# Crossbar DMA transposes from DRAM in place of TensorE transposes, and another last tile, in an eight-core conformer layer

## The chip, the cores and the metric

One program runs on the 8 cores of a Trainium2 chip. Each core has its own engines: TensorE (PE, with its weight loads as PEld), VectorE (DVE), ScalarE (ACT), GpSimd (POOL) and SyncE (SP), and 16 DMA engines that all queues share. The metric is the device time of the slowest core in microseconds (us); the median over the runs counts.

## The reference

One layer over `x` of shape (2, 8192, 1024):

```
u = rms_norm(x, g);  a_val | a_gate | q | k | v = u @ W_in
A = silu(layer_norm(conv31(a_val * sigmoid(a_gate))))        # 512 channels
B = attention(q, k, v)      # 8 heads x 64; a 64-frame chunk sees itself and the 8 chunks before it,
                            # with a learned bias by distance
x = x + rms_norm(concat(A, B) @ W_out)
f = (gelu(gate) * val) @ W_down,  gate | val = conv3(rms_norm(x) @ W_up)    # width 2816
x = x + rms_norm(f)
```

## The kernel before

Each core computes 2048 tokens and reads 640 tokens ahead of them again, so it holds 21 token tiles (`w` = 0 to 20) of 128 tokens. The tiles form groups `g`: 0 (tiles 0 to 3), 1 (tile 4), 2 (5 to 8), 3 (9 to 12), 4 (13 to 16) and 5 (17 to 20). Groups 2 to 5 are the core's own tokens.

The program has these stages. A start projects groups 0 to 2 while the weights arrive. Then come four attention slots, one for each group 2 to 5; in each, the 20 steps of the group's attention (`attn_steps`: scores, exponential, values) are woven with other work: normalizing and transposing the tiles of later groups (`prep_a`, `prep_b`), projecting them (`proj_a`, `proj_v`, `proj_k`, `proj_q`), the 31-wide convolution (`conv_units`), its layer norm (`ln_units`), and in the last slot the output projection of the first half (`wo_step`). Then the FFN runs in two halves `H`, each an up part (`ffn`) and a down part (`ffn_down`) over 8 tiles.

A matmul contracts over partitions, so activations must be channel-major before they meet a weight. Two places turn them. `prep_b(w)` takes the normalized tile `ub` (128 tokens x 1024 channels, bf16), does eight 128x128 TensorE transposes into a PSUM bank (L561) and one DVE copy into `uT` (L565). `fin(n)`, four per slot, takes the attention output of one token tile out of `atok`, does four TensorE transposes (L845) and one DVE copy into `aoT` (L849); `wo_mm` reads `aoT` as its stationary operand.

All operations are recorded with their reads and writes, and a list scheduler orders them for each engine by a priority, which is the order of recording, and by estimated durations. `weave` records the side work of a slot at given fractions of the attention steps; those pairs of numbers in `slot` set the order. The order is then fixed: each engine and each queue issues its instructions in that order and waits at each for its semaphores. SP issues nearly all plain DMAs (x tiles L498, the convolution's input out to DRAM and back as `hd`, L701 and L708, and others), one queue in one order; a DMA on SP whose source is not ready holds all that stand behind it.

The last tile of the second half has a routine of its own, `last()`: it multiplies the left 512 output columns over all 22 weights first (L1204), so that their squares (L1207) are taken while the right 512 columns run, and it sends the result as two halves on two queues (L1224). All other tiles go through `part` (both halves together, L1172) and `epi` (squares over 1024 columns L1188, two GpSimd operations for the reciprocal root, L532 and L535, two DVE operations L1191 and L1194, one DMA L1195).

Of the kernel before, what the change touches and what calls it, by code (L numbers as in the profile page):

```python
# [9 lines left out]
BF16 = mybir.dt.bfloat16  # L10
# [10 lines left out]
AFF = 0  # L21
AHEAD = 0
CWF = 0.8
# [297 lines left out]
def build_program():  # L321
# [23 lines left out]
    hd = {g: nc.dram_tensor("hd%d" % g, [8, 128, 4 * GS[g]], BF16).ap() for g in GS}  # L345
    CN = {0: 129, 1: 128}
# [3 lines left out]
    with ExitStack() as es:  # L350
# [17 lines left out]
        def pb(name, b0, nb=1, dt=F32):  # L368
# [6 lines left out]
            ["h1s", "wob"] + ["hd%d" % g for g in GS] + ["cd0", "cd1"])}  # L375
# [25 lines left out]
        assert o <= 16740, o  # L401

        uTb = {i: sb("uT%d" % i, 16740 + i * 8192, [8, 512], BF16) for i in range(2)}
        u2T = sb("u2T", 16740, [8, 1028], BF16)
        Wk = sb("Wk", 33188, [8, 512], BF16)
        Wv = sb("Wv", 41380, [8, 512], BF16)
        Wo = sb("Wo", 33188, [8, 1024], BF16)
        Wq = sb("Wq", 49572, [8, 512], BF16)
        coT = [sb("coT%d" % i, 49572, [4, 1032], BF16) for i in range(2)]
        sig = [sb("sig%d" % i, 57828 + i * 2048, [512]) for i in range(2)]  # L410
        hst = [sb("hst%d" % i, (61924, 153284)[i], [8, 4, 64], BF16) for i in range(2)]
# [7 lines left out]
        aoT = [sb("aoT0", 113316, [4, 1026], BF16), sb("aoT1", 57828, [4, 1024], BF16)]  # L419
# [13 lines left out]
        uT4 = sb("uT4", 195876, [8, 128], BF16)  # L433
# [36 lines left out]
        PL = [pb("PL%d" % i, 4 + i) for i in range(2)]  # L470
# [86 lines left out]
        def prep_b(w):  # L557
            u_ = ub[w % 3]
            b = nbank(True)
            for k in range(8):  # L560
# [3 lines left out]
            ut, j = uT_of(w)  # L564
            S.op("dve", lambda: dve.tensor_copy(out=ut.ap[:, :, j * 128:(j + 1) * 128],  # L565
                                                in_=b.apb.rearrange("p (k t) -> p k t", k=8)),
# [27 lines left out]
        def proj_v(g, j):  # L594
# [3 lines left out]
            for k in range(8):  # L598
                S.mm(lambda k=k: pe.matmul(b.ap, lhsT=ut.ap[:, k, j * 128:(j + 1) * 128], rhs=Wv.ap[:, k, :],  # L599
                                           start=(k == 0), stop=(k == 7)),  # L600
                     reads=[ut[j], Wv[(k, 0)]], writes=[b], last=(k == 7))
# [7 lines left out]
        def v_wide():  # L609

            bs = [nbank() for _ in range(5)]
            for k in range(8):
                for w in range(5):
                    ut, j = uT_of(w)
                    S.mm(lambda k=k, w=w, ut=ut, j=j: pe.matmul(bs[w].ap, lhsT=ut.ap[:, k, j * 128:(j + 1) * 128], rhs=Wv.ap[:, k, :],  # L615
# [11 lines left out]
        def k_wide():  # L627
# [3 lines left out]
            for k in range(8):  # L631
                for c in range(4):
                    S.mm(lambda k=k, c=c: pe.matmul(bs[c].ap, lhsT=Wk.ap[:, k, c * 128:(c + 1) * 128], rhs=ut.ap[:, k, :],
# [18 lines left out]
        def proj_k(g, c):  # L652
# [4 lines left out]
            for k in range(8):  # L657
                S.mm(lambda k=k: pe.matmul(b.ap[:, :N], lhsT=Wk.ap[:, k, c * 128:(c + 1) * 128], rhs=ut.ap[:, k, :N],  # L658
# [7 lines left out]
        def proj_q(g, c):  # L666
# [4 lines left out]
            for k in range(8):  # L671
                S.mm(lambda k=k: pe.matmul(b.ap[:, n0:N], lhsT=Wq.ap[:, k, c * 128:(c + 1) * 128], rhs=ut.ap[:, k, n0:N],  # L672
# [4 lines left out]
        def proj_a(g, c, part):  # L677
# [7 lines left out]
            for k in range(8):  # L685
                S.mm(lambda k=k: pe.matmul(b.ap[:, :n], lhsT=Wa.ap[:, k, col:col + 128], rhs=ut.ap[:, k, n0:N],  # L686
# [5 lines left out]
            else:  # L692
                s_ = n // 8
                S.op("dve", lambda: dve.scalar_tensor_tensor(
                    out=hs.ap[:, :, c, 0:s_], in0=sg.ap[:, :n].rearrange("p (s q) -> p q s", q=8), scalar=1.0,
                    in1=b.ap[:, :n].rearrange("p (s q) -> p q s", q=8), op0=ALU.add, op1=ALU.mult),
# [16 lines left out]
        def halo_units():  # L713
# [39 lines left out]
            def turn():  # L753
                b = nbank()
                for c in range(4):
# [3 lines left out]
                S.op("dve", lambda: dve.tensor_copy(out=aoT[0].ap[:, :, 0:2], in_=b.apb[:, 0:8].rearrange("p (c t) -> p c t", c=4)),  # L759
                     reads=[b], writes=[aoT[0][4]])  # L760
# [405 lines left out]
        def ffn_down(H):  # L1166
# [63 lines left out]
            for i in range(8):  # L1230
# [17 lines left out]
                if H and i == 7:  # L1248
                    last()
                    continue  # L1250
# [10 lines left out]
            if H == 0:  # L1261
                epi(7)
# [270 lines left out]
```

The softmax here doesn't subtract the row's maximum and nothing guards it: scores larger than these inputs give would overflow.

## Time and profile before

| what | value |
|---|---|
| median of 3 runs | 842.96 us (841.79 to 843.06) |
| the profiled execution | 841.79 us |
| span of its slowest core (core 3), first to last instruction | 840.7 us |
| spans of all cores | 834.7 to 840.7 us |
| PE busy | 790.6 us, 94% |
| DVE busy | 588.2 us, 70% |
| ACT busy | 499.9 us, 59% |
| POOL busy | 179.7 us, 21% |

The profiled execution took 1.1 us more than its span. Busy shares are averages over the whole span; the stages have different limits. The attention slots lie between about 65 and 335 us, the FFN from 335 us on.

### The profile page before, as it was taken

To read this page: it belongs to the slowest core of one execution; us is meant where nothing else is said; L and a number is where in the kernel's file an instruction comes from. 1 tells how busy PE (TensorE), PEld (TensorE's weight loads), DVE (VectorE), ACT (ScalarE), POOL (GpSimd) and SP (SyncE) were. 2 spreads that over 40 slices of the span, in tenths; PEclk is the share of its full clock that TensorE was granted. 3 is DMA by queue.
4 is the path that set the end of the run, shared out by engine and by line. 5 is a ranking of instruction groups with operands and counts; after the bars stand their busy time and mean duration, and the time that the engine had idled before them with its cause. 6 is when DMAs were issued, how large, how long until landed. Compare 5 with 4: busy or idle time off the path is not lost.

```text
span 840.7 us, 15580 instructions; the slowest of 8 cores (834.7 to 840.7 us)
## 1 busy us (share of the span) xinstructions
PE 790.6 (94%) x5324; PEld 420.1 (50%) x5324; DVE 588.2 (70%) x758; ACT 499.9 (59%) x764; POOL 179.7 (21%) x324
## 2 busy tenths in 40 slices
PE   1998998899998897999999999999999999999997
PEld 1545465554554445666666654444444444444443
DVE  2566477778757888889999984454488888885223
ACT  4567363525555787789888784323377777772111
POOL 3122121000003453232333311111222222200010
PEclk9999999999999999999999999999999999999999
DMA  8994778021637843599999995443398888811222
GB/s 258 310 292 133 126 151 101 27 44 9 127 92 129 166 157 102 60 101 107 111 113 114 181 147 159 153 161 139 126 153 78 78 76 80 77 15 50 102 101 101
DMA packets 145619, 101.00 MB, mean 120 GB/s; under 512 B 117122, under 2 KB 124674, under 8 KB 145156
## 3 DMA queue, kind: packets, MB, share of 16 engines
q0 software_dynamic: 95520, 31.37, 36.7%
q1 hardware_dynamic: 49444, 68.29, 27.8%
q8 instruction: 44, 0.72, 0.4%
q14 instruction: 35, 0.29, 0.1%
q10 hardware_dynamic: 576, 0.34, 0.1%
HBM read 110.31 MB, written 23.12 MB: 159 GB/s over the span
## 4 chain that ended last, share of the span: by engine, by line
PE 73%; DVE 13%; issue 7%; ACT 5%; DMA 1%; POOL 1%; DVEq 0%; ACTq 0%; POOLq 0%
PE ps L1277 24%; PE ps L1172 14%; PE ps L686 7%; PE ps L1088 5%; DVE big L1299 4%; DVE big L1302 4%; PE ps L672 3%; PE ps L599 3%; PE ps L658 3%; PE ps L920 2%; PE ps L790 2%; PE ps L826 2%; PE ps L615 1%; PE ps L1204 1%; PE ps L561 1%
## 5 line engine op out<-in xcount | busy, mean ns | idle before, releaser
L1277 PE MATMUL ps<-big 128*128 128x344 bf16 (+2 forms) x1760 | 310.9, 337 | 1.1 <-ACT big L1298 0.9
L1277 PEld LDWEIGHTS ps<-big 128*128 128x128 bf16 x1760 | 171.2, 98 | 139.8 <-issue 3.9
L1172 PE MATMUL ps<-big 128*128 128x512 bf16 x660 | 144.2, 378 | 0.0
L1299 DVE SCALAR_TENSOR_TENSOR big<-big 128x1026 f32<-128x1026 f32 (+1 forms) x88 | 113.0, 1285 | 20.3 <-ACT big L1289 11.2
L1163 POOL DMA_DIRECT2D big<-w_up x88 | 77.4, 880 | 213.0 <-PE ps L1277 192.4
L1302 DVE SCALAR_TENSOR_TENSOR big<-big 128x1026 f32<-128x1026 f32 (+1 forms) x88 | 113.3, 1288 | 9.4 <-DVE big L1299 0.7
L1294 ACT ACTIVATE big<-ps,big 128x1026 f32<-128x1026 f32 (+1 forms) x88 | 106.8, 1214 | 0.0
L1172 PEld LDWEIGHTS ps<-big 128*128 128x128 bf16 x660 | 63.7, 97 | 76.6
L801 ACT ACTIVATE big<-ps 128x1024 bf16<-128x1024 f32 x80 | 80.2, 1024 | 26.9 <-PE ps L790 22.3
L1088 PE MATMUL ps<-big 128*128 128x512 bf16 (+1 forms) x272 | 64.9, 391 | 2.1 <-DVE big L1036 2.1
L1290 ACT COPY big<-ps 128x1024 f32<-128x1024 f32 x44 | 44.6, 1015 | 36.1 <-PE ps L1277 36.0
L535 POOL TENSOR_TENSOR big<-big 128x1 f32<-128x1 f32 (+1 forms) x71 | 50.3, 710 | 71.3 <-DVE big L1105 55.4
L686 PE MATMUL ps<-big 128*128 128x512 bf16 (+1 forms) x320 | 61.4, 340 | 3.9 <-ACT big L690 1.8
L1191 DVE SCALAR_TENSOR_TENSOR big<-ps,big 128x1024 f32<-128x1024 f32 x15 | 19.3, 1285 | 62.7 <-POOL big L535 62.7
L532 POOL TENSOR_SCALAR big<-big 128x1 f32<-128x1 f32 (+1 forms) x53 | 16.7, 315 | 189.3 <-ACT big L1188 86.4
L1312 DVE TENSOR_TENSOR big<-big 128x1026 bf16<-128x1026 bf16 (+1 forms) x44 | 53.7, 1221 | 0.3 <-ACT big L1099 0.2
L1283 ACT COPY big<-ps 128x1032 f32<-128x1032 f32 x44 | 44.5, 1011 | 15.7 <-PE ps L1277 8.7
L1188 ACT ACTIVATE big<-ps 128x1024 bf16<-128x1024 f32 x15 | 15.3, 1023 | 57.9 <-PE ps L1172 57.9
L1309 ACT ACTIVATE big<-big 128x1026 bf16<-128x1026 f32 (+1 forms) x44 | 46.7, 1061 | 4.7 <-DVE big L1302 2.4
L813 POOL MEMSET big<- 64x128 bf16 x64 | 14.6, 229 | 147.4 <-ACT big L801 95.6
L1126 ACT ACTIVATE big<-big 128x1024 bf16<-128x1024 f32 (+1 forms) x17 | 18.0, 1061 | 46.4 <-DVE big L1114 46.0
L1088 PEld LDWEIGHTS ps<-big 128*128 128x128 bf16 (+1 forms) x272 | 25.9, 98 | 34.7 <-issue 6.3
(126 smaller groups left out, 934.2 us busy)
## 6 DMA issues: line engine op xcount, KB each, us to landing
big<-w_up POOLq DMA_DIRECT2D x88, 256.0 KB, 5.4
big<-xw SPq DMA_DIRECT2D x37, 512.0 KB, 6.6
big<-w_in SPq DMA_DIRECT2D x40, 256.0 KB, 12.3
h1s<-big SPq DMA_DIRECT2D x16, 512.0 KB, 2.9
big<-h1s SPq DMA_DIRECT2D x16, 512.0 KB, 5.1
out<-big SPq DMA_DIRECT2D x15, 512.0 KB, 2.9
big<-w_down POOLq DMA_DIRECT2D x22, 256.0 KB, 6.1
hd<-big SPq DMA_DIRECT2D x4, 512.0 KB, 3.4
```

The costliest lines, as they stand in the source:

```text
L535: S.op("pool", lambda: pool.tensor_tensor(out=stat.ap[0:n, out:out + 1], in0=stat.ap[0:n, tmp:tmp + 1], in1=nh.ap[0:n], op=ALU.pow), reads ...
L686: S.mm(lambda k=k: pe.matmul(b.ap[:, :n], lhsT=Wa.ap[:, k, col:col + 128], rhs=ut.ap[:, k, n0:N], start=(k == 0), stop=(k == 7)), reads=ut ...
L801: S.op("act", lambda: act.activation(out=p_.ap, in_=s_.ap, func=AF.Exp), reads=[s_], writes=[p_], n=1024)
L1088: S.mm(lambda k=k, half=half, l_=l_, b=b: pe.matmul(b.ap[0:n], lhsT=l_, rhs=Wo.ap[:, k, half * 512:(half + 1) * 512], start=(k == 4), stop ...
L1163: S.dma("pool", "wup%d" % (si % NWR), lambda: pool.dma_start(out=wring[si % NWR].ap, in_=w_up_v[:, :, cbk * 128:(cbk + 1) * 128]), writes= ...
L1172: S.mm(lambda f=f, half=half, i=i: pe.matmul((PH[2] if i % 2 else PD).ap[:, half, :], lhsT=actb[f].ap[:, i * 128:(i + 1) * 128], rhs=Wd[f] ...
L1277: S.mm(lambda k=k, t=t, c0=c0, n_=n_: pe.matmul(pu.ap[:, t, 0:n_], lhsT=wb.ap[:, k, :], rhs=u2T.ap[:, k, c0:c0 + n_], start=(k == 0), stop ...
L1294: S.op("act", lambda: act.activation(out=tav, in_=pv, func=AF.Identity, scale=fdw.ap[:, cbk, 2:3], bias=fdw.ap[:, cbk, 3:4]), reads=[pu, f ...
L1299: S.op("dve", lambda: dve.scalar_tensor_tensor(out=tbv, in0=xv[1], scalar=fdw.ap[:, cbk, 1:2], in1=tav, op0=ALU.mult, op1=ALU.add), reads= ...
L1302: S.op("dve", lambda: dve.scalar_tensor_tensor(out=tav, in0=xv[0], scalar=fdw.ap[:, cbk, 0:1], in1=tbv, op0=ALU.mult, op1=ALU.add), reads= ...
L1309: S.op("act", lambda: act.activation(out=av_, in_=tav, func=AF.Gelu_apprx_tanh), reads=[ta], writes=[actb[j]], n=1026)
L1312: S.op("dve", lambda: dve.tensor_tensor(out=av_, in0=av_, in1=tav, op=ALU.mult), reads=[ta, actb[j]], writes=[actb[j]], n=1026)
```

## The change

Four things change together.

1. `prep_b` of tiles 9 to 20 (groups 3 to 5, `TD = 9`) no longer uses PE and DVE. SP stores the normalized tile to a DRAM tensor `ud` (256 KB) and then reads it back with one DMA crossbar transpose into `uT`. Tiles 0 to 8 stay as they were.
2. `fin` runs once per head pair instead of once per token tile: SP stores the 512 x 128 outputs of that pair to a DRAM tensor `at` (128 KB) and reads them back with a crossbar transpose into `aoT`, which is now one buffer per group. There are 16 such pairs.
3. So that a transposed tile lands in one piece, `uT` is laid out by tile, then channel block, then token. The moving operand of `proj_k`, `proj_q` and `proj_a` is now four runs of 128 elements in place of one run of 512.
4. `last()` is gone: the last tile goes through `part` and `epi` like the others.

Smaller edits: of each four `affine` operations of the first layer norm two go to ACT (`AFF = 2`); every second `proj_a` product is read in order and written strided instead of the other way round; and the fractions in `slot` are all new.

```diff
-AFF = 0
+AFF = 2
+TD = 9
+TKB = 768
...
-        uTb = {i: sb("uT%d" % i, 16740 + i * 8192, [8, 512], BF16) for i in range(2)}
+        uTb = {i: sb("uT%d" % i, 16704 + i * 8192, [4, 8, 128], BF16) for i in range(2)}
...
         def prep_b(w):
             u_ = ub[w % 3]
+            ut, j = uT_of(w)
+            if w >= TD:
+                S.dma("sp", "ud%d" % (w % 3), lambda: sp.dma_start(out=ud[w], in_=u_.ap), reads=[u_], writes=[DH["ud%d" % w]], kb=256)
+                S.dma("sp", "ut%d" % (w % 3), lambda: sp.dma_start_transpose(out=ut.ap[:, j, :, :], in_=ud[w]),
+                      reads=[DH["ud%d" % w]], writes=[ut[j]], kb=TKB)
+                return
             b = nbank(True)
...
-                S.mm(lambda k=k: pe.matmul(b.ap[:, :N], lhsT=Wk.ap[:, k, c * 128:(c + 1) * 128], rhs=ut.ap[:, k, :N],
+                S.mm(lambda k=k: pe.matmul(b.ap[:, :N].rearrange("p (a b) -> p a b", b=128), lhsT=Wk.ap[:, k, c * 128:(c + 1) * 128], rhs=ut.ap[:, :, k, :],
...
+                o_, r_ = hs.ap[:, :, c, 0:s_], "p (s q) -> p q s"
+                if c % 2:
+                    o_, r_ = o_.rearrange("p q s -> p s q"), "p (s q) -> p s q"
...
-            def fin(n):
-                b = nbank()
-                for c in range(4):
-                    S.mm(lambda c=c: pe.transpose(out=b.apb[:, c * 128:(c + 1) * 128],
-                                                  in_=atok.ap[:, n - n0, c * 128:(c + 1) * 128], identity=ident.ap),
-                         reads=[atok[h_] for h_ in range(4)] + [ident], writes=[b], last=(c == 3), n=140)
...
+            def fin(hp):
+
+                S.dma("sp", "ao%d" % (hp % 2), lambda: sp.dma_start(out=atd[g, hp].rearrange("(n p) c -> p n c", p=128),
+                                                                    in_=atok.ap[:, :, hp * 128:(hp + 1) * 128]),
+                      reads=[atok[hp]], writes=[DH["at%d%d" % (g, hp)]], kb=192)
+                S.dma("sp", "at%d" % (hp % 2), lambda: sp.dma_start_transpose(out=aoT[g].ap[:, hp, :], in_=atd[g, hp]),
+                      reads=[DH["at%d%d" % (g, hp)]], writes=[aoT[g][hp]], kb=TKB / 2)
...
-                if H and i == 7:
-                    last()
-                    continue
...
-                         (pa_units(1) + pa_units(2), 0, 0.19), (prep_units(3), 0.061, 0.179),
...
+                         (pa_units(1) + pa_units(2), 0, 0.19), (prep_units(3), 0.066, 0.288),
...
```

What this does to the order is seen on two engines. The rows are those of the program, not of a trace: a line number, an operation, its tiles and how often it repeats. First SP's queue at the start of the slot of group 2, before; `xw` are x tiles, `cvp` and `fdw` small constants, `hd` the convolution's input (the 128x8x16 and 128x32x4 forms are those of group 1).

```order
L514 DMA big<-w_in 128x512 x8
L498 DMA big<-xw 128x1024 x3
L1385 DMA big<-cvp 128x96
L1388 DMA big<-fdw 128x176
L498 DMA big<-xw 128x1024
L701 DMA hd<-big 128x8x16
L708 DMA big<-hd 128x32x4
L498 DMA big<-xw 128x1024 x3
```

The same queue in the changed kernel, from the end of the small constants on. The first row's two transposes are those of tiles 9 and 10, the next that of tile 11, the last that of tile 12.

```order
L566 DMA_TRANSPOSE big<-ud 128x8x128 x2
L712 DMA hd<-big 128x8x16
L566 DMA_TRANSPOSE big<-ud 128x8x128
L502 DMA big<-xw 128x1024
L565 DMA ud<-big 128x1024
L502 DMA big<-xw 128x1024
L565 DMA ud<-big 128x1024
L502 DMA big<-xw 128x1024
L565 DMA ud<-big 128x1024
L719 DMA big<-hd 128x32x4
L566 DMA_TRANSPOSE big<-ud 128x8x128
```

Between the store of group 1's convolution input and its way back (L712 and L719) there are now a transpose, three x loads and three stores, and the transpose of tile 12 stands behind all of them. The stores of tiles 9 to 11 and the two small constants come ahead of these rows.

Now PE, where group 3's tiles are first used; before, L686 is `proj_a` (L694 after), L561 the transposes of `prep_b`, L790 and L826 scores and values (L801 and L837 after), L741 the values of the halo (L752 after). Before, the last row below holds the last 8 matmuls of group 2 and all 64 of group 3.

```order
L686 MATMUL ps<-big 128x512 x16
L561 MATMUL ps<-big 128x128 x8
L826 MATMUL ps<-big 128x65 x4
L790 MATMUL ps<-big 128x512 x2
L790 MATMUL ps<-big 128x128 x2
L790 MATMUL ps<-big 128x384 x2
L686 MATMUL ps<-big 128x512 x16
L561 MATMUL ps<-big 128x128 x8
L826 MATMUL ps<-big 128x65 x8
L686 MATMUL ps<-big 128x512 x72
```

In the changed kernel group 2's last 8 `proj_a` matmuls come in the fourth row; L607 is `proj_v`, on tiles 9 and 10, and the last row is `proj_a` on group 3, which reads all four tiles.

```order
L694 MATMUL ps<-big 128x512 x56
L752 MATMUL ps<-big 2x65 x20
L837 MATMUL ps<-big 128x65 x8
L752 MATMUL ps<-big 2x65 x20
L694 MATMUL ps<-big 128x512 x8
L837 MATMUL ps<-big 128x65 x8
L767 MATMUL ps<-big 128x2 x4
L801 MATMUL ps<-big 128x512 x2
L801 MATMUL ps<-big 128x128 x2
L801 MATMUL ps<-big 128x384 x2
L837 MATMUL ps<-big 128x65 x8
L607 MATMUL ps<-big 128x512 x16
L694 MATMUL ps<-big 128x512 x16
```

The transposes are gone from PE, and 16 `proj_v` matmuls and the halo's values now stand ahead of group 3's first `proj_a`.

## Rows read from the trace of the kernel before

**Rows 1.** The page's chain that ended last: shares of the span by engine.

```profile
PE 73%; DVE 13%; issue 7%; ACT 5%; DMA 1%; POOL 1%; DVEq 0%; ACTq 0%; POOLq 0%
```

**Rows 2.** Busy us by engine in four stretches (PE, PEld, DVE, ACT, POOL), clock, DMA.

```profile
65.00:160.00 95.00, 86.27 (x908) 50.98 (x907) 60.29 (x104) 52.86 (x82) 17.21 (x47) 0.98 0.59 107
160.00:220.00 60.00, 59.55 (x433) 30.15 (x431) 49.13 (x110) 26.41 (x36) 2.72 (x13) 1.00 0.21 45
220.00:262.00 42.00, 40.38 (x418) 24.49 (x415) 26.14 (x47) 21.58 (x32) 2.04 (x10) 1.00 0.52 115
262.00:335.30 73.30, 62.03 (x602) 33.61 (x596) 60.98 (x109) 56.73 (x93) 35.30 (x59) 0.94 0.65 141
```

**Rows 3.** Timeline of PE in slots 2 and 3: start us, us, engine, line.

```profile
91.10 15.85 PE L686 MATMUL ps<-big 128*128 128x512 bf16 x72 [1.02 <-ACT big L690]
...
157.75 0.40 PE L845 MATMUL ps<-big 128*128 128x128 bf16 x4
157.99 0.61 PE L561 MATMUL ps<-big 128*128 128x128 bf16 x8
158.43 0.40 PE L826 MATMUL ps<-big 128*128 128x65 bf16 x8
...
180.13 1.90 PE L599 MATMUL ps<-big 128*128 128x512 bf16 x8
181.87 1.90 PE L686 MATMUL ps<-big 128*128 128x512 bf16 x8
```

**Rows 4.** Groups by line: busy us, mean ns of one, idle before.

```profile
L845 PE MATMUL ps<-big 128*128 128x128 bf16 x64 | 5.4, 219 | 3.0 <-DVE big L1102 1.4 <-DVE big L849 1.1 <-ACT big L675 0.5
```

**Rows 5.** Timeline of SP's queue in the slot of group 2.

```profile
69.89 0.42 SPq L1388 DMA_DIRECT2D big<-fdw  x1
...
80.70 0.64 SPq L708 DMA_DIRECT2D big<-hd  x1
```

**Rows 6.** The eight loads of `wob` (256 KB each, one row of 2 KB per partition).

```profile
DMA to landing us min/median/max: 2.8/6.2/7.2
```

**Rows 7.** The five loads of `hd` (four of 512 KB in runs of 128 B).

```profile
DMA to landing us min/median/max: 6.4/7.4/9.4
```

**Rows 8.** The page's DMA issues: KB each, median us to landing.

```profile
out<-big SPq DMA_DIRECT2D x15, 512.0 KB, 2.9
big<-hd SPq DMA_DIRECT2D x1, 32.0 KB, 6.4
```

**Rows 9.** Timeline of the end: tile 14's `epi`, then `last()`.

```profile
825.50 9.66 PE L1204 MATMUL ps<-big 128*128 128x512 bf16 x44
826.16 1.03 ACT L1188 ACTIVATE big<-ps 128x1024 bf16<-128x1024 f32 x1 [8.68 <-PE ps L1172]
...
831.31 0.34 SPq L1195 DMA_DIRECT2D out<-big  x1
...
835.30 0.60 ACT L1207 ACTIVATE big<-ps 128x512 bf16<-128x512 f32 x1 [4.00 <-PE ps L1204]
...
838.62 0.35 ACTq L1224 DMA_DIRECT2D out<-big  x1
```

**Rows 10.** Groups by line, shapes kept apart, on DVE and ACT.

```profile
L565 DVE COPY big<-ps 128x1024 bf16<-128x1024 bf16 x21 | 14.2, 689 | 11.0 <-PE ps L561 11.0
L849 DVE COPY big<-ps 128x512 bf16<-128x512 bf16 x16 | 6.3, 422 | 5.5 <-PE ps L845 5.1
L694 DVE SCALAR_TENSOR_TENSOR big<-big,ps 128x512 bf16<-128x512 f32 x16 | 17.3, 1079 | 18.7 <-PE ps L686 16.5 <-ACT big L551 1.1 <-PE ps L826 1.0
L837 DVE TENSOR_TENSOR big<-ps,big 128x512 bf16<-128x512 f32 x16 | 11.0, 685 | 0.4
L997 DVE TENSOR_SCALAR big<-big 128x129 f32<-128x129 f32 x32 | 9.4, 343 | 0.0
L994 ACT ACTIVATE big<-big 128x128 f32<-128x128 f32 x32 | 14.2, 493 | 4.5 <-DVE big L987 4.5
```

**Rows 11.** PE and PEld busy us of line L561 alone, in one stretch.

```profile
160.00:220.00 60.00, 0.97 (x15) 0.72 (x12) 1.00 0.21 45
```

More of the change, by code:

```diff
@@ L345, in build_program @@
     hd = {g: nc.dram_tensor("hd%d" % g, [8, 128, 4 * GS[g]], BF16).ap() for g in GS}
+    ud = {w: nc.dram_tensor("ud%d" % w, [128, D], BF16).ap() for w in range(TD, NT)}
+    atd = {(g, c): nc.dram_tensor("at%d%d" % (g, c), [512, 128], BF16).ap() for g in range(2, 6) for c in range(4)}
     CN = {0: 129, 1: 128}
@@ L374, in build_program @@
         DH = {k: Buf(S, "dram", k, i, i + 1, None) for i, k in enumerate(
-            ["h1s", "wob"] + ["hd%d" % g for g in GS] + ["cd0", "cd1"])}
+            ["h1s", "wob"] + ["ud%d" % w for w in range(TD, NT)] + ["at%d%d" % (g, c) for g in range(2, 6) for c in range(4)] + ["hd%d" % g for g in GS] + ["cd0", "cd1"])}
         pe, act, dve, pool, sp = nc.tensor, nc.scalar, nc.vector, nc.gpsimd, nc.sync
@@ L400, in build_program @@
         hc = const("hc", [44, 2])
-        assert o <= 16740, o
-        uTb = {i: sb("uT%d" % i, 16740 + i * 8192, [8, 512], BF16) for i in range(2)}
[L404 to L411, printed above, removed]
+        assert o <= 16700, o
+        uTb = {i: sb("uT%d" % i, 16704 + i * 8192, [4, 8, 128], BF16) for i in range(2)}
+        u2T = sb("u2T", 16700, [8, 1028], BF16)
+        Wk = sb("Wk", 33148, [8, 512], BF16)
+        Wv = sb("Wv", 41340, [8, 512], BF16)
+        Wo = sb("Wo", 33148, [8, 1024], BF16)
+        Wq = sb("Wq", 49532, [8, 512], BF16)
+        coT = [sb("coT%d" % i, 49532, [4, 1032], BF16) for i in range(2)]
+        sig = [sb("sig%d" % i, 57788 + i * 2048, [512]) for i in range(2)]
+        hst = [sb("hst%d" % i, (61884, 153284)[i], [8, 4, 64], BF16) for i in range(2)]
         kvs = {i: (sb("ks%d" % i, 66020 + i * 8256, [4, 512], BF16), sb("vs%d" % i, 70116 + i * 8256, [4, 8, 65], BF16)) for i in range(3)}
@@ L469, in build_program @@
         PH = [pb("PH%d" % i, 2 * i, 2) for i in range(3)]
-        PL = [pb("PL%d" % i, 4 + i) for i in range(2)]
         PD = pb("PD", 6, 2)
@@ L867, in attn_steps @@
             out += [lambda: av(len(steps) - 2), lambda: av(len(steps) - 1)]
-            fins = [lambda n=n: fin(n) for n in range(n0, n1 + 1)]
-            return out, fins
+            return out
         def weave(steps, lists):
@@ L1446, in slot @@
             else:
-                lists = [([(3.5, lambda t=t: wo_step(t)) for t in range(WS, 9 + 5)], 0.161, 0.5), (one(lambda: conv_stats(1)), 1, 1),
+                lists = [([(3.5, lambda t=t: wo_step(t)) for t in range(WS, 9 + 5)], 0.428, 0.828), (one(lambda: conv_stats(1)), 0.797, 0.797),
                          ([(1, lambda k=k: ln1.sub(k)) for k in range(8)], 1, 1)]
-            weave(st_ + fins, lists)
+            weave(st_, lists)
         def wo_step(t):
```

87 lines of the change are left out of this document (27 added, 60 removed).

## Prediction

> **What bounds the kernel now.** I read the chain that ended last first: 73% of the span is PE work, and DVE comes next with 13% [rows 1]. So PE time that is taken away counts only where PE is the one that is waited for, and that differs by stage. The busy times by stretch show where [rows 2]. From 160 to 220 us PE is busy 59.55 of 60 us, from 220 to 262 us 40.38 of 42: each matmul taken out there should shorten the span by its whole length. From 65 to 160 us it is 86.27 of 95. From 262 to 335 us, the output projection beside the last group's attention, it is 62.03 of 73.3, with DVE at 60.98 and ACT at 56.73: no engine is full, and what is saved there is saved in part. Together PE stands still for 22 us of the 270 (270.3 less 248.2, the sum of the four). The FFN behind them is not touched, except for its very end.
>
> **The transposes that leave PE.** 12 tiles of `prep_b` with eight transposes each, and 16 `fin` with four. A PE row's own length overlaps the next, so I take the distance from start to start: eight transposes from 157.99 to 158.43, 0.44 us, and four from 157.75 to 157.99, 0.24 us [rows 3]. That is 12 x 0.44 = 5.3 and 16 x 0.24 = 3.8, in sum 9.1 us. As a second reading, the 64 `fin` transposes have 5.4 us of busy time, with 3.0 us of waits just before them [rows 4]; the busy time counts overlap, and waits mostly move to the next instruction, so I claim neither. Four of the 16 `fin` lie in the stretch from 262 us, where PE is not full; for these 1.0 us I count half. Term: **-8.6 us**.
>
> **The DVE copies that go with them.** 12 x 0.689 and 16 x 0.422 us, 15.0 us [rows 10]. Of the layer norm's 32 `affine` operations 16 go from DVE (343 ns) to ACT (493 ns): 5.5 us less on DVE, 7.9 more on ACT, which in the stretch they come from, 160 to 220 us, is busy 26.41 of 60 us [rows 2, 10]. The `proj_a` products take 1079 ns for 128x512 where a dense product of that size out of PSUM takes 685; with the strided side moved from reading to writing, 8 of 16 may gain up to 0.39 us each, or lose as much. DVE thus has 20 us less to do, give or take 3, of 196.5 in these stretches. Where PE is full that is worth nothing, and where it isn't, the order decides; I take 0, and a gain as a rival.
>
> **The moving operand in four runs.** No matmul in this trace reads its moving operand in separate runs, so I bound it. Eight matmuls of 512 columns start every 1.74 us (180.13 to 181.87), 218 ns each; eight of 128 columns take 0.44 us, 55 ns each [rows 3]. Four runs charged as four separate matmuls would be 220 ns. The bounds are 0 and 2 ns for each of some 550 matmuls, 1 us in all; I take 0.
>
> **The new DMAs.** 12 stores of 256 KB and 16 of 128 KB, as many transposes back, all on SP. A store of 512 KB lands after 2.9 us [rows 8], so the stores are short. No crossbar transpose is in the trace. From below it costs what a plain load of 256 KB does at best, 2.8 us; from above, what 512 KB in runs of 128 B takes at worst, 9.4 us [rows 6, 7]. Its source is in rows of 2 KB, as in the first, its destination in pieces of 256 B, nearer to the second. I take 5 us for `prep_b` and half for `fin`.
>
> What matters is when the tiles are needed. The attention outputs have time: `wo_mm` reads groups 2 and 3 only in the last slot, and groups 4 and 5 in the FFN. Groups 4 and 5 of `uT` are needed a slot later. Tight is group 3. Before, its first `proj_a` comes eight matmuls after 91.10 us, at 92.8; after, 16 `proj_v` matmuls come ahead of it (3.5 us; the halo's values, also ahead now, about cancel against the transposes that are gone), so all four tiles must have landed by about 96 us. The first two transposes stand on SP behind the constants, which wait for weights and end at 69.89 + 0.42 = 70.3 us [rows 5]. If one transpose runs at a time, the fourth lands at 70.3 + 4t, in time for t up to 6.4 us. By the other way, tile 12's transpose stands behind group 1's `hd` load, which was issued at 80.70 + 0.64 and takes 6.4 us [rows 5, 8]: 87.7 + t, in time up to t = 8.3. With 5 us nothing waits there. But x loads, stores and the `hd` transfers now share one queue with transposes that wait for a store to land, and ACT and DVE wait for x tiles in their own fixed order; I add **+1 us** for that, between 0 and the 12 us of the rival below.
>
> Here the Trainium skill gives two answers. "Advanced Engine Details and Errata", X-Bar Transpose (TRN2), says that such DMAs run about as fast as plain ones, at 350 to 400 GB/s; by it a tile would take the 2.8 us of the lower bound, and the term would be 0. "VectorE: DVE Perf Modes", The three transpose paths, gives 1309 ns for a 128x128 block by crossbar against 390 on TensorE, and its rules prefer TensorE where PSUM may be the destination; eight blocks in turn would be an estimated 10.5 us per tile, and the slow rival below would come out another 4 us later. No run here shows either.
>
> **The last tile.** Before, the last matmul ends at 825.50 + 9.66 = 835.16; the squares of the right half start at 835.30, and the span ends at 840.7: 5.4 us. After, the last tile takes the way of tile 14: from the start of its squares (826.16) to its DMA (831.31) are 5.15 us, and 512 KB land 2.9 us later: 8.05 us [rows 8, 9]. The same matmuls run either way. Nothing covers this, since it is the end. Term: **+2.65 us**.
>
> **The sum.** -8.6 + 0 + 0 + 1 + 2.65 = -4.95 us against the profiled execution's own 841.8 us (span 840.7, and 1.1 around it) gives 836.8. The median shown is 1.2 above that execution, so a median run should take **838 us**, 0.6% less.
>
> **Rivals.** The measurement of this kernel can tell about 0.2% (1.7 us) from no change, so "same" is 841.3 to 844.6.
>
> *The sum holds* (chance 0.45; 834 to 841). For it: PE is full in half of the stretches and close to it in another.
>
> *The transposes are slow, and the kernel is slower* (0.27). The place is group 3's first `proj_a`, the mechanism SP's queue: four transposes must land between 70.3 and 96 us. Each us by which t exceeds 6.4 costs 4 us there; without waits the change gains 5.95, so from t = 6.4 + 5.95 / 4 = 7.9 us on it is a loss. At t = 9.4 the fourth lands at 107.9, PE waits 11.9 us, and the sum is -8.6 + 2.65 + 11.9 = +6, 849 us by the median. For it: the destination is in small pieces, as in the rows of 6.4 to 9.4 us. Against it: those moved twice the bytes.
>
> *The gain is larger* (0.15). DVE loses some 20 of 196.5 us and the new fractions place the side work otherwise; if a third of the 22 us in which PE stands still goes too, the time is 838 - 7 = 831 us. For it: the stretch from 262 us, where DVE is as busy as PE. Against it: there only four copies leave DVE, 1.7 us.
>
> *The gain goes into other waits* (0.13). PE issues in a fixed order; where it was close to starving, it arrives earlier at an instruction whose ACT, DVE or DMA input is no earlier. If the stretches 65 to 160 and 262 to 335 us keep their length, only the 60 and 42 us between them shrink, by what lies there: some 15 transposes of `prep_b`, 0.97 us of busy time [rows 11], and four `fin`, 1.0 us. The end's 2.65 us takes that back and more: 843.6 us.
>
> **Chances and range.** Faster by over 0.2%: the first and third, 0.60. Within 0.2%: the fourth and the edges of its neighbours, 0.14. Slower: most of the second, 0.26. The range reaches down into the larger gain, 830, and up to the slow transposes at the longest row I have, 849; outside remain about 0.05 below and 0.13 above. The likeliest case has 834 to 841 for itself.
>
> **What would show it.** Right: no PE transposes after about 66 us but those of `wo_tp` and the halo; the FFN's first matmul at 327 to 330 us in place of 335.3; transposes that land 3 to 6 us after their issue; the first `proj_a` of group 3 waiting for nothing, or for less than 2 us; 512-column projections still every 218 ns; the end 8 us after the last matmul. Wrong: PE idle before `proj_v` or `proj_a` with a DMA as its releaser; ACT or DVE idle at `prep_a` for an x tile; SP waiting for a store while an x load or `hd` stands behind; or projections visibly over 218 ns, which would make the four runs a cost of their own.

## The result: 15 us slower, and where the time stands in the profile after

The changed kernel takes 857.42 us (median; 857.23 to 857.56), beside 842.38 for the kernel before in the same session: ratio 1.0178, 95% interval 1.0158 to 1.0198. The forecast was 838 us with a range of 830 to 849, so both the sign and the range were wrong. A few executions were disturbed, whatever the kernel; the comparisons leave them out, and f5 below keeps only two.

Line numbers change: `proj_v`, `proj_k`, `proj_q`, `proj_a` are L607, L666, L680, L694; the `proj_a` product is L705, softmax products L818, values L837, the convolution L928, the FFN's up part L1251. Two lines that the prediction did not speak of matter most. `late_vectors` loads three norm weights on SP and multiplies them by 32 on DVE; `cast_wo` has GpSimd issue eight casts of `w_out` from fp32 to bf16, DRAM to DRAM (`wob`, L1053; 4 MB read, 2 MB written):

```python
S.dma("sp", "c_g2", lambda: sp.dma_start(out=g2b.ap, in_=gvec_d[2:3, :].partition_broadcast(128)), writes=[g2b])   # L1366
S.op("dve", ... g2b.ap, scalar1=32.0 ..., reads=[g2b], writes=[g2b])                                            # L1368
S.dma("pool", "wob%d" % k, ... wob[k * 128:(k + 1) * 128, :], in_=w_out_d[...], reads=[gmp], ..., cast=True)     # L1053
```

First, busy time by stretch of the changed kernel, columns as in [rows 2], the same borders but for the last.

```profile
65.00:160.00 95.00, 74.35 (x633) 38.37 (x636) 44.27 (x75) 44.81 (x69) 16.25 (x46) 0.87 1.00 179
160.00:220.00 60.00, 52.68 (x457) 29.55 (x456) 52.58 (x90) 29.23 (x48) 2.27 (x12) 1.00 0.36 64
220.00:262.00 42.00, 40.73 (x331) 21.84 (x332) 24.01 (x44) 21.52 (x36) 1.64 (x8) 1.00 0.42 90
262.00:346.00 84.00, 71.42 (x730) 40.73 (x736) 67.53 (x124) 65.70 (x107) 33.33 (x64) 0.96 0.72 159
```

From 65 to 160 us PE was idle for 8.7 us before and is now idle for 20.7, and the granted clock fell from 0.98 to 0.87. The DMA engines went from 0.59 busy to 1.00. The finer windows of that stretch have the hole in the second row: 12 us without one matmul, and after it the clock at 0.69.

```profile
119.00:135.00 16.00, 15.59 (x137) 7.42 (x134) 6.08 (x13) 9.79 (x12) 5.63 (x15) 1.00 1.09 174
135.00:147.00 12.00, 0.00 (x0) 0.00 (x0) 1.11 (x3) 0.34 (x1) 0.17 (x1) 0.64 0.99 122
147.00:155.00 8.00, 7.94 (x57) 4.05 (x58) 1.35 (x4) 1.70 (x3) 0.24 (x1) 0.69 0.59 56
```

The timeline of several engines there (start us, us, engine, line, and in brackets the idle time before and what ended it) names the chain.

```profile
119.04 1.34 SPq L1366 DMA_DIRECT2D big<-gvec  x1
120.01 1.58 POOL L1053 DMA_DIRECT2D wob<-w_out  x3 [1.40 <-DVE big L1367]
...
122.18 0.96 POOL L1053 DMA_DIRECT2D wob<-w_out  x2 [0.23 <-issue]
124.20 1.44 POOL L1053 DMA_DIRECT2D wob<-w_out  x3 [0.23 <-issue]
...
131.17 16.95 SPq L856 DMA_DIRECT2D at<-big  x1
...
145.89 0.69 DVE L1368 TENSOR_SCALAR big<-big 128x1024 f32<-128x1024 f32 x1 [14.45 <-DMA big<-gvec]
147.06 0.60 PE L837 MATMUL ps<-big 128*128 128x65 bf16 x8 [12.47 <-DVE big L818]
```

DVE issues in a fixed order, and between two softmax products stands the multiplication of the constant `g2b`. It waits 14.45 us for the constant's load, issued at 119.04; the next softmax products, and the values on PE, wait behind it. Nobody needs `g2b` before the output projection, over 100 us later.

These rows are core 0, the slowest. In four of the eight cores (3, 5, 6 and 7) the constant landed sooner, after 12.7 to 16.5 us, and DVE waited at most 4.2 us for it; there PE stood 10.5 to 14.1 us for another load, the convolution's `hd`. So already in this run it is not always the same load that is waited for. Core 3:

```profile
152.51 3.74 PE L928 MATMUL ps<-big 128*128 128x129 bf16 x33 [10.47 <-DMA big<-hd]
```

The three constants' loads, first in the kernel before, then in the changed one, core 0 again: SP's time for the issue (ns), when it was issued, and the landing.

```profile
L1391 SPq DMA_DIRECT2D big<-gvec x1: 328/328/328, 117.9 to 117.9; - x1
L1395 SPq DMA_DIRECT2D big<-gvec x1: 328/328/328, 122.2 to 122.2; - x1
L1392 SPq DMA_DIRECT2D big<-gvec x1: 328/328/328, 161.0 to 161.0; - x1
...
DMA to landing us min/median/max: 3.6/3.8/5.6
```

```profile
L1365 SPq DMA_DIRECT2D big<-gvec x1: 713/713/713, 105.0 to 105.0; - x1
L1369 SPq DMA_DIRECT2D big<-gvec x1: 339/339/339, 116.8 to 116.8; - x1
L1366 SPq DMA_DIRECT2D big<-gvec x1: 1342/1342/1342, 119.0 to 119.0; - x1
...
  DVE big L1368: 14.5, 1
...
DMA to landing us min/median/max: 5.3/7.1/26.8
```

Before, the casts were issued from 125.1 us on, behind the first two loads, and had landed when the third was issued at 161.0; the DVE row that needs it came at 166.14.

```profile
L1045 POOL DMA_DIRECT2D wob<-w_out x8: 486/489/616, 125.1 to 129.8; - x8
...
DMA to landing us min/median/max: 6.1/11.6/16.2
```

```profile
166.14 0.69 DVE L1394 TENSOR_SCALAR big<-big 128x1024 f32<-128x1024 f32 x1
```

Now the third load is issued 1 us ahead of the casts, and in core 0 it lands with the last of them (issued by 125.6, 20.5 us to landing).

The rows also show what lets the load go. The buffer of `g2b` is that of an x tile as well, and the load is issued right behind the last `prep_a` on DVE, at 160.96 behind a row that ends at 160.89 before, at 119.04 (above) behind one that ends at 118.46 in the changed kernel.

```profile
160.15 0.74 DVE L554 TENSOR_SCALAR big<-big 128x1024 bf16<-128x1024 f32 x1
160.96 0.33 SPq L1392 DMA_DIRECT2D big<-gvec  x1
```

```profile
117.72 0.74 DVE L558 TENSOR_SCALAR big<-big 128x1024 bf16<-128x1024 f32 x1
```

The `proj_a` product, every second one now written with a stride, answers to its row in [rows 10] (1079 ns): the group, then one row of either form.

```profile
L705 DVE SCALAR_TENSOR_TENSOR big<-big,ps 128x512 bf16<-128x512 f32 x16 | 28.1, 1754 | 19.6 <-PE ps L694 14.1 <-PE ps L837 5.4
```

```profile
79.17 1.08 DVE L705 SCALAR_TENSOR_TENSOR big<-big,ps 128x512 bf16<-128x512 f32 x1 [2.22 <-PE ps L694]
82.62 2.43 DVE L705 SCALAR_TENSOR_TENSOR big<-big,ps 128x512 bf16<-128x512 f32 x1 [1.72 <-PE ps L694]
```

The transposes themselves, from issue to landing, 256 KB and then 128 KB, with SP's time for an issue as the first figures:

```profile
L566 SPq DMA_TRANSPOSE big<-ud x12: 1231/1572/5501, 68.4 to 160.6; - x12
...
DMA to landing us min/median/max: 3.5/4.6/8.9
```

```profile
L859 SPq DMA_TRANSPOSE big<-at x16: 1128/1156/7905, 106.8 to 349.2; - x16
...
DMA to landing us min/median/max: 2.4/3.3/10.8
```

### The profile page after: what moved, and what is told of

The parts are those of the page before. It is cut to its first block, busy times and chain, and to the rows that moved or that the text cites. A ratio compares the mean times of both kernels' runs of the same rounds, so it can differ in the third digit from the quotient of the medians.

```text
span 856.2 us, 15330 instructions; the slowest of 8 cores (853.1 to 856.2 us)
## 1 busy us (share of the span) xinstructions
PE 783.8 (92%) x5116; PEld 412.6 (48%) x5164; DVE 579.6 (68%) x711; ACT 503.9 (59%) x778; POOL 175.3 (20%) x325
## 4 chain that ended last, share of the span: by engine, by line
PE 60%; DVE 15%; issue 8%; DMA 6%; ACT 5%; SPq 4%; POOL 1%; DVEq 0%; ACTq 0%; POOLq 0%
PE ps L1251 22%; PE ps L1180 15%; PE ps L694 6%; PE ps L1096 5%; DVE big L1273 4%; DVE big L1276 4%; DMA big<-gvec 3%; PE ps L680 2%; SPq L518 2%; PE ps L607 2%; PE ps L666 2%; PE ps L801 2%; PE ps L837 2%; PE ps L928 2%; DMA big<-w_in 1%
## 5 line engine op out<-in xcount | busy, mean ns | idle before, releaser
L1251 PE MATMUL ps<-big 128*128 128x344 bf16 (+2 forms) x1746 | 310.8, 338 | 1.9 <-ACT big L1272 0.5
L1251 PEld LDWEIGHTS ps<-big 128*128 128x128 bf16 x1760 | 171.7, 98 | 140.7 <-issue 4.0
L1180 PE MATMUL ps<-big 128*128 128x512 bf16 x689 | 154.2, 381 | 0.8
L1273 DVE SCALAR_TENSOR_TENSOR big<-big 128x1026 f32<-128x1026 f32 (+1 forms) x88 | 113.1, 1285 | 23.1 <-ACT big L1263 11.6
L1180 PEld LDWEIGHTS ps<-big 128*128 128x128 bf16 x704 | 68.4, 98 | 83.0 <-issue 2.3
L694 PE MATMUL ps<-big 128*128 128x512 bf16 (+1 forms) x320 | 62.1, 347 | 6.2 <-ACT big L529 2.5
L539 POOL TENSOR_TENSOR big<-big 128x1 f32<-128x1 f32 x71 | 47.3, 668 | 65.5 <-DVE big L1113 57.0
L837 PE MATMUL ps<-big 128*128 128x65 bf16 x640 | 32.3, 198 | 16.5 <-DVE big L818 14.6
L694 PEld LDWEIGHTS ps<-big 128*128 128x128 bf16 x320 | 26.4, 100 | 37.9 <-issue 12.3
```

The source lines that it names most:

```text
L539: S.op("pool", lambda: pool.tensor_tensor(out=stat.ap[0:n, out:out + 1], in0=stat.ap[0:n, tmp:tmp + 1], in1=nh.ap[0:n], op=ALU.pow), reads ...
L694: S.mm(lambda k=k: pe.matmul(b.ap[:, :n].rearrange("p (a b) -> p a b", a=ut.ap.shape[1]), lhsT=Wa.ap[:, k, col:col + 128], rhs=ut.ap[:, :, ...
L837: S.mm(lambda n=n, first=first, lastmm=lastmm, hh=hh, h=h, o_=o_, a=a, vb=vb, kj=kj: pe.matmul(ob[hh].ap[:, (n - n0) * 65:(n - n0) * 65 + 65],
L1180: S.mm(lambda f=f, half=half, i=i: pe.matmul((PH[2] if i % 2 else PD).ap[:, half, :], lhsT=actb[f].ap[:, i * 128:(i + 1) * 128], rhs=Wd[f] ...
L1251: S.mm(lambda k=k, t=t, c0=c0, n_=n_: pe.matmul(pu.ap[:, t, 0:n_], lhsT=wb.ap[:, k, :], rhs=u2T.ap[:, k, c0:c0 + n_], start=(k == 0), stop ...
L1273: S.op("dve", lambda: dve.scalar_tensor_tensor(out=tbv, in0=xv[1], scalar=fdw.ap[:, cbk, 1:2], in1=tav, op0=ALU.mult, op1=ALU.add), reads= ...
```

## The experiments

Ratios are to the kernel before, run on the same chip in the same session; between kernels of different sessions the ratios count more than the medians. The expectations of e1, e2, e5 and e6 call the constant of L1368 `gfp`; it is `g2b` (`gfp` is L1369 and L1370). Where they say `gfp`, they mean "the constant that DVE stands for", and e1 therefore moved another one than it was meant to.

**e1_gfp_late.** Only `gfp` is multiplied late.

```diff
+        def scale_gfp():
+            S.op("dve", ... gfp.ap ..., reads=[gfp, coT[0][(3, 65)]], writes=[gfp], n=512)
...
+                         (one(load_wo), 0.412, 0.412), (one(scale_gfp), 0.7, 0.7), ...
```

> Only the multiplication of the constant gfp by 32 is moved on VectorE, from the middle of group 3's softmax multiplications to group 5's slot; its load and every other transfer stay. Theory A (one constant): TensorE's idle time at 135-147 us is VectorE standing 14.5 us before this multiplication, for a load that took 26.75 us in full queues. Then the 12.5 us of TensorE's wait goes, and with it the rows at half clock behind it: 857 becomes 842 to 847. Theory B (backlog): the queues are full anyway, and another row (the load of hd, the output transposes) waits there next: 853 to 857.

860.74 us, 1.0195 (1.015 to 1.024). With the wrong constant moved it says nothing on theory A: DVE stood 18.6 us before L1368 as ever.

**e2_one_form.** Every `proj_a` product reads with the stride again.

```diff
-                if c % 2:
+                if False:
                     o_, r_ = o_.rearrange("p q s -> p s q"), "p (s q) -> p s q"
```

> Only proj_a's product on the odd channel blocks is put back to the form of the even ones (read with a stride, written in rows). Its 512-column rows take 2.43 us in the changed kernel, and 1.07 in the other form: 8 rows, 11 us of VectorE's time between 80 and 120 us. Theory A with the constant alone as the cause: VectorE has slack there and the wait for gfp ends when the load lands: 856 to 858. Theory C (the slow form is on the path): TensorE waits for it twice for 2.1 us and starts the slot late: 850 to 854.

859.43 us, 1.0169 (1.0127 to 1.0212): no gain. Another constant (L1370) was now waited for, 25.8 us in the slowest core, and PE stood longer: 11.0 to 24.2 us over the eight cores, 17.7 in the mean, where the longest stand of each core in the changed kernel is 7.6 to 14.1 us, 11.6 in the mean. So this run can't tell what the form is worth. What it costs without the stall is shown by f1 below.

**e5_u_by_pe** and **e6_out_by_pe.** First the edit of e5, then that of e6 (the old `fin`, on the new `aoT`).

```diff
-TD = 9
+TD = 21
```

```diff
-            def fin(hp):
+            def fin(n):
+                b = nbank()
+                for c in range(4):
+                    S.mm(lambda c=c: pe.transpose(...
+                S.op("dve", lambda: dve.tensor_copy(out=aoT[g].ap[:, :, (n - n0) * 128:(n - n0 + 1) * 128], ...
...
+            weave(st_ + fins, lists)
```

> The normalized x of groups 3 to 5 is turned by TensorE again (12 tiles, 8 transposes each, and a VectorE copy); the outputs stay with the DMA. 12 stores and 12 transposes of 256 KB leave SP's queue between 83 and 162 us. Theory A1 (these transfers fill the queue in front of gfp): its load lands in under 10 us, VectorE's wait goes and 12 us come back, less the 4 to 9 us that the transposes cost TensorE: 848 to 855. Theory B1 (the queue is full from the loads of hd and the casts of w_out, not from these): the wait stays and TensorE's work is added: 859 to 866.

> The attention outputs are turned by TensorE again (16 tiles, 4 transposes each and a VectorE copy, at the end of each slot); the normalized x stays with the DMA. 16 stores and 16 transposes of 128 KB leave SP's queue, of which two pairs lie ahead of gfp's landing (issues that held SP for 7.91 and 16.95 us). Theory A2 (the issues of the output transfers hold SP and so gfp): the constant lands in time: 846 to 852, 12 us back less 3 to 4 us of transposes. Theory A1 (the normalized x does it): VectorE's wait is still 10 us or more: 857 to 862.

867.4 us, 1.0266 (1.0228 to 1.0304), and 865.97 us, 1.0255 (1.0216 to 1.0294). Both times lie above all the ranges expected. Neither replaced part is the cause alone. e6 kept the stall (17.6 us, A1's side). e5 had none at 135 us but one later, in rows that gave the next theory away. Its timeline, and who waited for the constants:

```profile
154.49 3.98 POOL L1053 DMA_DIRECT2D wob<-w_out  x8 [5.78 <-DVE big L1367]
...
163.06 0.33 SPq L1369 DMA_DIRECT2D big<-gvec  x1
```

```profile
  DVE big L1370: 16.2, 1
...
DMA to landing us min/median/max: 3.7/4.7/16.0
```

No normalized x goes by DMA here; but again the load is issued among the casts' transfers, and takes 16 us. All three constants' loads come later here, at 137.6, 163.1 and 181.2 us in place of 105.0, 116.8 and 119.0: with the tiles back on TensorE the last `prep_a` is late again (180.43 us).

**e7_wob_late.** The casts also read the `q` of group 4, so they are issued at 226.8 us instead of about 120.

```diff
-                      reads=[gmp], writes=[DH["wob"][k]], kb=512, cast=True)
+                      reads=[gmp, g_q(4)[3]], writes=[DH["wob"][k]], kb=512, cast=True)
...
-                lists = [..., (one(cast_wo), 0.599, 0.599), ...
+                lists = [..., (one(cast_wo), 1, 1), ...
```

> The eight casts of w_out to DRAM are issued after group 4's last proj_q (some 50 us later) instead of at 117 to 125 us; the constants' loads and their multiplications stay where they are. In four kernels run so far the constant for which VectorE stood landed within 2 us of the last cast (145.8 beside 145.6 in the changed kernel). Theory W (the casts, in flight together with the new transfers, hold the constant): the load of g2b lands in under 12 us, VectorE's wait of 14.5 us goes: 842 to 848. Theory Q (SP's own queue, with the stores and transposes ahead, holds it): the wait stays at 8 us or more: 853 to 860.

845.94 us, 1.0006 (0.998 to 1.0033): 1.7% back, 14.5 us. The constants landed after 6.3/6.5/7.4 us (minimum, median, maximum) and DVE waited for none. Theory W holds, Q falls.

**e10_consts_late** and **e12_consts_wob** (that and the late casts). Both multiplications go to the slot of group 4.

```diff
+        def scale_late():
+            S.op("dve", ... g2b.ap ..., reads=[g2b, coT[0][(3, 65)]], writes=[g2b], n=512)
+            S.op("dve", ... gfp.ap ..., reads=[gfp, coT[0][(3, 65)]], writes=[gfp], n=512)
...
+                         (one(load_wo), 0.412, 0.412), (one(scale_late), 0.7, 0.7), ...
```

> Both late constants (g2b and gfp) are multiplied by 32 in group 5's place, where they are first needed, not between group 3's softmax multiplications; all transfers stay. In the run before this one only gfp was moved, and VectorE stood as long for g2b. Theory A (VectorE's fixed order behind a late constant is the whole stall): 842 to 848. Theory B (the queues are so far behind that another row takes the wait, first the load of hd before the convolution): the idle time of TensorE at 135-150 us only moves: 853 to 858.

> Both edits together: the constants multiplied late, and the casts of w_out issued some 50 us later. If either edit alone takes the whole stall away (A and W), this is equal to the better of the two within 1.5 us: 841 to 847. If the constants' wait hides a second wait on the queues (B), this is better than either by 4 us or more: 840 to 846, with the others at 850 or above.

862.41 us, 1.021 (1.0155 to 1.0266), and 846.3 us, 1.0016 (0.9991 to 1.0042). With the constants out of the way another load takes the wait, as theory B had it (the time is above its 853 to 858); in the list of waits (us in all, times, longest) it is the one that feeds the convolution, as in cores 3, 5, 6 and 7 of the changed kernel:

```profile
PE ps L928 <- DMA big<-hd: 16.6, 1, 16.6
```

So the cause is not the one constant, but whatever load is needed while the casts are in flight. e12 is as e7: with the casts away the constants' place costs nothing.

**f4_before_casts_155.** The counter-test: the kernel before, the casts only moved to just ahead of its third constant's load. The order of PE, DVE, ACT and SP is the same; only GpSimd's differs.

```diff
-                      reads=[gmp], writes=[DH["wob"][k]], kb=512, cast=True)
+                      reads=[gmp, g_q(3)[3]], writes=[DH["wob"][k]], kb=512, cast=True)
```

> The kernel before, with nothing transposed by DMA; only the eight casts of w_out wait until group 3's last proj_q is done, so that they are issued at about 155 to 160 us, just ahead of the load of g2b at 161.0 us, for which VectorE's row at 166.14 us has only some 1 us of slack. Theory W (the casts alone hold a constant issued beside them): the load lands in 10 us or more in place of 3.8, VectorE stands for 5 to 12 us there: 847 to 853. Theory Q (casts and the new transfers are both needed to fill the queues; here they carry 0.06 of their time): it lands in under 6 us and the time stays at 841 to 844.

858.93 us, 1.0165 (1.0146 to 1.0185), above theory W's 847 to 853: a loss as large as the change's, with no transpose by DMA in it. Its timeline, the constants' landing, and two windows, the load's flight and the time after PE's stand:

```profile
156.72 1.11 POOL L1045 DMA_DIRECT2D wob<-w_out  x2 [2.62 <-ACT big L675]
157.97 0.96 POOL L1045 DMA_DIRECT2D wob<-w_out  x2
160.00 2.45 POOL L1045 DMA_DIRECT2D wob<-w_out  x4 [0.23 <-issue]
...
161.47 0.33 SPq L1392 DMA_DIRECT2D big<-gvec  x1
...
179.59 0.70 DVE L1394 TENSOR_SCALAR big<-big 128x1024 f32<-128x1024 f32 x1 [12.86 <-DMA big<-gvec]
182.55 3.57 PE L686 MATMUL ps<-big 128*128 128x512 bf16 x8 [12.04 <-DVE big L694]
```

```profile
DMA to landing us min/median/max: 3.8/6.0/18.0
```

```profile
161.50:179.50 18.00, 8.56 (x56) 3.93 (x54) 4.24 (x6) 3.25 (x4) 1.35 (x4) 0.85 0.87 125
182.50:190.00 7.50, 7.45 (x51) 5.13 (x52) 2.67 (x6) 0.60 (x1) 0.17 (x1) 0.66 0.01 2
```

The same load takes 18.0 us where it took 3.8 behind empty queues; in each of the eight cores it lands within 0.3 us of the last cast. While it is in flight the DMA engines are 0.87 busy. PE stands for 12 us, and its next eight matmuls take 3.57 us in place of 1.9: after 12 us without a matmul it works near the lower of its two levels (1.2 of 2.4 GHz), and over the next 7.5 us the granted clock is 0.66. That is an estimated 2.5 us on top of the 12.0, 14.5 in all, as the medians have it (858.93 beside 844.48).

**f1_wob_form** (e7 and one form of the product) and **f2_wob_form_last** (that and `last()` back).

> The changed kernel with the late casts, and proj_a's product on the odd channel blocks put back to the form of the even ones. Without the stall at 135 us the 8 rows of 2.43 us are no longer hidden behind it. Theory C (the slow form is on the path: TensorE waited 1.03 us for it three times): 2 to 4 us less than with the late casts alone (845.9): 842 to 844. Rival (VectorE has slack between 80 and 120 us): 845 to 847.

> As the run with the late casts and one form of the product, and the last down tile put back to column halves. The time from the FFN's first matmul to the end was 505.7 us over the cores before and 507.8 with the late casts, so the last tile is worth 2 us, with 2.65 predicted: 839.5 to 842. Rival (the tail hides it, as the run with last() alone, 858.1, would have it): no difference, 842 to 845.

839.25 us, 0.9933 (0.9915 to 0.995), and 835.05 us, 0.9901 (0.9879 to 0.9924), both below their ranges. Against e7 the form alone is worth 0.73% or 6 us, give or take 3; every engine has the same order in both. The `proj_a` product in f1, beside 28.1 us in the group above:

```profile
L705 DVE SCALAR_TENSOR_TENSOR big<-big,ps 128x512 bf16<-128x512 f32 x16 | 17.2, 1077 | 21.4 <-PE ps L694 11.0 <-PE ps L837 6.0 <-ACT big L555 4.4
```

In core 0 of e7 PE waited three times for about 1 us behind such a product, at 86.4, 110.5 and (through the layer norm queued on DVE) 182.9 us; group 3's last `proj_a` ended at 116.1 us there, and at 111.3 in f1. f1 and f2 are both faster than the kernel before, f2 by 1%. `last()` is worth 4.2 us by the medians, 2.7 by the ratios, give or take 2.

**e3_last_back.** Only `last()` back in the changed kernel.

```diff
+                if H and i == 7:
+                    last()
+                    continue
```

> Only the last down tile is put back to column halves (last()); all else is the changed kernel. The prediction had 2.65 us for it, on the end of the chain whatever stands ahead: 854 to 855.5 beside 857.4. Rival: the time from the FFN's first matmul to the end grew by 4.8 us; if all of it hangs on the last tile, 851.5 to 853.5.

858.12 us, 1.0153 (1.010 to 1.0206), no gain that can be told: its runs take 855.4 to 861.5 us, and the stall differs by several us from core to core. But from the FFN's first matmul to the end, the mean over the eight cores of the profiled execution is 505.7 us before, 508.1 in the changed kernel, 506.0 here.

**f3_group3_pe.** f2 with group 3's tiles on TensorE.

```diff
-TD = 9
+TD = 13
```

> As the run before it in this list, and the four tiles of group 3's normalized x are turned by TensorE again; groups 4 and 5 and the outputs stay with the DMA. Theory H (the removed transposes left a hole: TensorE stood 5.19 us at 64 us for the cast weights, and its clock then fell to 0.60 in 67 to 84 us, with 0.90 before): the four tiles' 1.8 us of transposes cost nothing, the clock is kept and four pairs of 256 KB leave the queue: 836 to 840. Rival (the hole is set by the weights' loads alone and the transposes are added to the path): 842 to 845.

842.99 us, 0.9977 (0.996 to 0.9993): 8 us lost for four tiles by the medians, 6 by the ratios. The time is in the rival's range and theory H falls. In its core 0 the clock was 0.50 from 70 to 80 us (0.53 in f2), so the transposes did not keep it.

**g0_form_last** (f2 with the casts at their own place) and **g1_small_casts** (g0 with each cast as two of 128 rows of 512 elements).

```diff
-... lambda k=k: pool.dma_start(out=wob[k * 128:(k + 1) * 128, :], in_=w_out_d[k * 128:(k + 1) * 128, :]),
+... lambda k=k: [pool.dma_start(out=wob[k * 128:(k + 1) * 128, c:c + 512], in_=w_out_d[...c:c + 512]) for c in (0, 512)],
```

> The changed kernel with one form of the product and last() back; the casts at their own place. Against 835.05 with the casts late. Theory W: the whole stall is here, 12 us of idle TensorE and the half clock behind it: 849 to 855. Rival (the slow form had made the collision, by shifting the order): 836 to 842.

> As g0_form_last, and each of the eight casts is issued as two of 128 rows of 512 elements in place of one of 16 rows of 8192; bytes, place and order of the engines stay. Theory P (long pieces: a load's small packets stand behind 8 KB pieces on every engine): the constant lands in under 12 us and the time falls to 836 to 843. Theory V (volume: 4 MB read and 2 MB written have to pass): as g0, within 3 us. A third way: GpSimd takes twice as long to issue sixteen casts, which holds the memsets of the softmax: up to 4 us more than g0.

850.3 us, 1.0109 (1.0091 to 1.0126): in the mended kernel the casts' place is worth 2.1%, 17 us (15 by the medians). g1: 853.9 us, 1.0141 (1.0116 to 1.0165), no gain. The packets did become shorter (2295 on the casts' queue from 114 to 150 us in place of 256, for 2.1 MB either way). Who waited for the constants, and their landing, in the slowest core of g0 and then of g1:

```profile
  DVE big L1405: 19.5, 1
  DVE big L1403: 1.0, 1
...
DMA to landing us min/median/max: 8.6/9.3/24.4
```

```profile
  DVE big L1403: 13.2, 1
  DVE big L1405: 12.4, 1
...
DMA to landing us min/median/max: 7.8/15.7/22.7
```

With short pieces the load that took 24.4 us (L1404) takes 15.7, but the next one (L1401), issued at 129.4 us while the casts are still under way, takes 22.7. The wait is split over two constants and no shorter in all. Theory P asked for under 12 us and falls; the time agrees with volume and with GpSimd's double issues, which this run doesn't separate. The Trainium skill, "DMA: Bandwidth & Descriptors", Queues, rings and completion order, says that an engine takes turns between queues and drains a whole packet before it switches; by that alone, a load would share the engines with the casts, and come sooner when their packets are shorter. The 15.7 us agree with that, the 22.7 us do not. That a load beside the casts is held is shown (16.0 us in e5, 18.0 in f4); why it is held for so long stays open.

**f5_outputs_only** (f2 with `TD = 21`) and **f6_x_only** (f2 with `fin` on TensorE).

> The version at 835.05 with all normalized x turned by TensorE again (12 tiles): only the attention outputs go by DMA. By the prediction's terms, 12 x 0.44 us of the 9.1 us come back: 839 to 842. Rival from the run with group 3 alone on TensorE (843.0, 8 us more for 4 tiles): the copies and the order cost more than the transposes: 844 to 850.

> The version at 835.05 with the attention outputs turned by TensorE again (16 tiles at the ends of the slots): only the normalized x goes by DMA. By the prediction's terms, 16 x 0.24 us come back: 837.5 to 840. Rival: the outputs' transposes need the last normalization of each slot, and TensorE waits there: 842 to 848.

f5: 844.2 and 844.0 us, beside 840.2 to 842.9 before, with no interval. f6: 842.82 us, 1.0018 (1.0007 to 1.0029). Either half alone gains nothing, and both together (f2) gain 8 us on the kernel before. The fractions in `slot` belong to the whole change, and the order moves with either edit; whether the transposes or the order make the difference was not tried.

## Why the prediction was wrong, step by step

**The step that failed first is "The new DMAs", +1 us.** I asked when the transposed tiles are needed, and costed the other traffic on the queue with 1 us. The first part held: transposes of 256 KB landed after 3.5/4.6/8.9 us where I took 5 (those of 128 KB after 3.3 in the median, where I took 2.5), group 3's first `proj_v` came at 95.30 us and its `proj_a` behind it, with no DMA as the releaser. So the rival "the transposes are slow" did not happen, though its sign came true. What I left out is that the change moves *other* loads: the third constant from 161.0 to 119.04 us, beside eight casts from GpSimd's queue that I had not looked at. The trace of before had what was needed: the casts at 125 to 130 us with up to 16 us to landing, a load at 161.0 and the DVE row that needs it at 166.14. f4 shows that this pair is fragile without the change. It cost 14.5 us (e7) to 17 (g0 against f2), where my term was 1. The load is earlier because the last x tile is read earlier (the `prep_a` rows above), and that comes with the transposes of the normalized x on DMA: with these tiles back on TensorE the third load is issued at 181.2 us (e5) and at 163.5 (f5, beside 120.5 in f2). What in them makes it so is argued from the code: `prep_a` of tile 20 writes the buffer `ub` of tile 17, which is now free once it is stored, and before was held until its transposes could write a `uT` buffer that group 3 still used.

**The `proj_a` product.** "May gain up to 0.39 us each, or lose as much" was bounded by the dense row of 685 ns. The strided write took 2.43 us, 1.36 more than the strided read; 8 rows make 10.9 us of DVE time, and 6 us of the kernel's (f1 against e7). A dense row bounds a gain; it says nothing on how far a stride can lose. So "DVE thus has 20 us less to do" became 8.6 (588.2 to 579.6); with one form, in f1, it is 17.2 (571.0).

**What held.** No transposes on PE but those of the first nine tiles, of the halo and of `wo_tp`. The moving operand in four runs costs nothing: eight 512-column matmuls of `proj_q` take 1.89 us, those of the projections in [rows 3] 1.90. The last tile: its squares begin at 847.99 us and the span ends at 856.2, 8.2 us where I had 8.05; the FFN stage is 2.4 us longer in the mean of the cores (508.1 less 505.7), predicted 2.65. That agreement is in part luck: such means of single executions differ by more between kernels with the same end (508.2 in f4, 504.5 in f5, both with `last()`).

**The sum without the two.** With the casts late and one form, but the tail as in the change, the ratio is 0.9933; the prediction's 836.8 on its own 841.8 us is 0.9941. In f2 the FFN's first matmul starts at 325.1 us in the mean of the cores, 331.9 before: 6.8 us, where -8.6 + 1 was forecast. So the total of the other terms came out. That the transposes were priced rightly one by one is not shown: the new fractions in `slot` are part of the change in f1 and f2, and by the prediction's terms f5 should give back 5.3 us and f6 3.8, where they gave back 8 to 9 us by the medians (844.1 and 842.8 beside 835.05) and some 10 by the ratios. To that extent the agreement may be luck.

**The two answers of the Trainium skill.** The Trainium skill's "Advanced Engine Details and Errata", X-Bar Transpose (TRN2), by which a tile would take the 2.8 us of a plain load, is nearer to the 4.6 us measured than the 10.5 us estimated from the Trainium skill's "VectorE: DVE Perf Modes", The three transpose paths. The transposes' own time was thus not what went wrong.

## What to carry to other kernels

When a change adds DMA traffic or frees a buffer earlier, list every load whose issue moves, the engine that waits for it in a fixed order, and what other queues carry at that time; a load with 1 us of slack became a stall as soon as a bulk transfer stood beside it (f4). Put such bulk transfers where nobody waits for a load, and test it by moving the bulk transfer, not the one that waits: moving the waiting row only gave the stall to the next load (e10). When a strided access changes sides, measure it; a dense row of the trace bounds the gain and not the loss.

## What the runs showed of the hardware

A load of one constant (512 KB written) took 18.0 us instead of 3.8 beside eight DRAM-to-DRAM casts, while the DMA engines were 0.87 busy (f4); with the casts under way they were 0.83 busy in the kernel before too (125 to 146 us), where nobody waited for a load. The strided write of bf16 from VectorE took 2.43 us for 128x512, the strided read 1.08, and another product of that size with nothing strided 0.69 [rows 10]. A crossbar transpose held SP for 1.2 and 1.6 us an issue in the median (128 and 256 KB), the plain DMAs of the same stage for 0.4 to 0.6. SP was also held 16.95 us for one plain issue at 131.17 us, with the casts under way.
